# A state-space scan in a two-layer decoder trunk: VectorE leaves the odd states of six rows incomplete, and TensorE adds what they lack in a second readout

## The reference, cut to what matters

```python
def _s5_glu(h, a_re, a_im, log_dt, b_re, b_im, c_re, c_im, d_skip, w_glu):
    ...
    bu = jnp.einsum('bsgc,gpc->bsgp', u.astype(jnp.complex64), B_bar)
    a = jnp.broadcast_to(A_bar, bu.shape)
    ...
    _, states = lax.associative_scan(combine, (a, bu), axis=1)
    y = jnp.einsum('bsgp,gcp->bsgc', states, C_mat).real.reshape(B, S, D)
    y = y + d_skip.astype(f32) * h.astype(f32)
    z = jax.nn.gelu(y).astype(h.dtype)
    val, gate = jnp.split(z @ w_glu, 2, axis=-1)
    return val * jax.nn.sigmoid(gate)
```

## Time and profile before

| what | us |
|---|---|
| three runs | 2299.93, 8127.71, 2298.12; median 2299.93 |
| the profiled execution | 2300.47 |
| its span, first to last instruction | 2298.7 |
| TensorE busy | 2257.9 |
| VectorE busy | 1681.7 |
| ScalarE busy | 1031.0 |
| serial part of the mixer with TensorE idle, longest wait | 6.90 |

### The profile page before, as it was taken

One profiled execution on the slowest core, in us unless ns is written; L12 is line 12 of the kernel. 1 busy time (PEld: TensorE's weight loads), 2 busy tenths in 40 slices (PEclk: granted clock), 3 DMA queues, 4 the chain that ended last, 5 costly groups with the idle time before them and its releaser, 6 DMA issues.

```text
span 2298.7 us, 34669 instructions
## 1 busy us (share of the span) xinstructions
PE 2257.9 (98%) x11966; PEld 1875.8 (82%) x11966; DVE 1681.7 (73%) x2549; ACT 1031.0 (45%) x1158; POOL 226.3 (10%) x324
## 2 busy tenths in 40 slices
PE   9999999999999999999998899999999999999997
PEld 7888888888888888888777788888888888888886
DVE  5685758778889878788889766676677654577666
ACT  4445546444444334444342544644455433444442
POOL 1000069701111111000100000000000000000000
PEclk9999999999999999999999899999999999999999
DMA  7655365678787777666765455665665665566664
GB/s 246 200 181 180 102 231 176 215 251 270 258 270 237 254 246 234 223 223 217 256 247 185 141 193 194 214 227 192 199 191 187 200 194 194 196 189 193 194 192 137
DMA packets 134490, 478.49 MB, mean 208 GB/s; under 512 B 15968, under 2 KB 19296, under 8 KB 133232
## 3 DMA queue, kind: packets, MB, share of 16 engines
q1 hardware_dynamic: 120432, 427.35, 56.4%
q0 software_dynamic: 13808, 49.64, 6.9%
q10 hardware_dynamic: 144, 0.07, 0.0%
HBM read 457.85 MB, written 19.14 MB: 208 GB/s over the span
## 4 chain that ended last, share of the span: by engine, by line
PE 92%; DVE 5%; issue 1%; DMA 1%; ACT 0%; POOL 0%; SPq 0%; DVEq 0%; ACTq 0%
PE ps L389 29%; PE ps L390 29%; PE ps L391 29%; DMA s_bt_raw<-in_s_bt 1%; PE ps L766 1%; PE ps L742 1%; PE ps L433 1%; DVE w_lo L1155 1%; PE ps L405 0%; PE ps L403 0%; PE ps L404 0%; DVE gated L1569 0%; DVE gated L1864 0%; DVE scan_wide L1917 0%; DMA res<-in_x 0%
## 5 line engine op out<-in xcount | busy, mean ns | idle before, releaser
L1155 DVE TENSOR_TENSOR w_lo<-raw,w_hi 128x1024 fp32r<-128x1024 f32 x771 | 945.5, 1232 | 506.9 <-ACT w_hi L809 500.4
L809 ACT ACTIVATE w_hi<-raw 128x1024 fp32r<-128x1024 f32 x771 | 813.3, 1059 | 967.8 <-PE ps L391 835.6
L389 PE MATMUL ps<-w_hi,x_hi 128*128 128x512 f32 x2304 | 901.6, 391 | 2.0 <-DVE x_lo L1989 1.8
L391 PE MATMUL ps<-w_hi,x_lo 128*128 128x512 f32 x2304 | 897.8, 390 | 0.0
L390 PE MATMUL ps<-w_lo,x_hi 128*128 128x512 f32 x2304 | 897.5, 390 | 0.0
L389 PEld LDWEIGHTS ps<-w_hi,x_hi 128*128 128x128 f32 x2304 | 433.0, 188 | 92.3 <-issue 2.8
L391 PEld LDWEIGHTS ps<-w_hi,x_lo 128*128 128x128 f32 x2304 | 433.0, 188 | 90.9
L390 PEld LDWEIGHTS ps<-w_lo,x_hi 128*128 128x128 f32 x2304 | 433.2, 188 | 88.5
L389 PE MATMUL ps<-w_hi,hid_hi 128*128 128x512 f32 x656 | 256.8, 391 | 1.8 <-DVE w_lo L1155 1.7
L390 PE MATMUL ps<-w_lo,hid_hi 128*128 128x512 f32 x656 | 255.5, 389 | 0.0
L391 PE MATMUL ps<-w_hi,hid_lo 128*128 128x512 f32 x656 | 255.3, 389 | 0.0
(11 more groups left out here) (302 smaller groups left out, 1426.7 us busy)
## 6 DMA issues: line engine op xcount, KB each, us to landing
raw<-in_w_inA SPq DMA_DIRECT2D x192, 512.0 KB, 4.3
raw<-in_w_inB SPq DMA_DIRECT2D x160, 512.0 KB, 4.1
raw<-in_w_outA SPq DMA_DIRECT2D x96, 512.0 KB, 3.5
raw<-in_w_outB SPq DMA_DIRECT2D x80, 512.0 KB, 4.1
raw<-in_w_in SPq DMA_DIRECT2D x64, 512.0 KB, 4.4
raw<-in_w_gate SPq DMA_DIRECT2D x64, 512.0 KB, 3.5
raw<-in_w_glu SPq DMA_DIRECT2D x64, 512.0 KB, 3.6
raw<-in_w_out SPq DMA_DIRECT2D x32, 512.0 KB, 3.3
```

The costliest lines, as they stand in the source:

```text
L389: pe.matmul(o, hi[:, kt + k, cols], WH[:, s, k, 0:width], start=(kt + k == 0), stop=False)
L391: last = pe.matmul(o, lo[:, kt + k, cols], WH[:, s, k, 0:width], start=False, stop=(kt + k == depth - 1))
L809: act.activation(WH[:, s, :, 0:width], RAW[:, s, :, 0:width], ACT.Copy).then_inc(hi_ready, 1)
L1155: dve.tensor_tensor(WL[:, s, :, 0:width], RAW[:, s, :, 0:width], WH[:, s, :, 0:width].bitcast(F32), ALU.subtract).then_inc(lo_ready, 1)
```

## The change

For rows 0 to 5 the third step of `grow` is dropped. The second step, which summed the two parts in place, writes its sum to a buffer of its own instead, `odd_carry` (`ODD`, 31 slots x 8 numbers for each of six rows). `read_out` of such a row no longer waits for `grown` before its 32 calls; it waits for the even states alone, reads `states` out with the odd slots as they are, then waits for the row's sum in `odd_carry`, and makes 32 further calls with the same tables, 31 columns each, which add into every second column of the row's place in PSUM from the fourth slot on. Rows 6 to 15 are as before. `odd_carry` lies at offset 184 KB, where the table `s_k` lies. A new semaphore, `direct_done`, is therefore raised by the last matmul of L754, and VectorE waits for it ahead of the first pair. `grown_before(pair)` gives the new count: four steps for each of the first three pairs, six for the others.

```diff
+        ODD = at("odd_carry", [P, 6, 2, 4, SLOTS // 2 - 1], 184)
...
+        def grown_before(pair):
+
+            return 4 * min(pair, 3) + 6 * max(pair - 3, 0)
...
+            last.then_inc(direct_done, 1)
 
             def read_out(row):
 
                 pe.wait_ge(ts_in[row % 14], 32 if 2 <= row < 14 else 48 if row < 2 else 64)
-                pe.wait_ge(grown, 6 * (row // 2) + 5 + row % 2)
+                carried = row < 6
                 pe.wait_ge(even_out, row + 1)
+                if not carried:
+                    pe.wait_ge(grown, grown_before(row // 2) + 5 + row % 2)
                 for s in range(SUB):
                     for ri in range(2):
                         for a in range(4):
                             last = pe.matmul(outputs(row, a, s, s + 1), TS[row % 14][:, a, ri, PW * s:PW * (s + 1)],
-                                             ST[:, row, ri, a, :], start=False, stop=(ri == 1), skip_group_check=True)
+                                             ST[:, row, ri, a, :], start=False, stop=(ri == 1 and not carried), skip_group_check=True)
+                if carried:
+                    pe.wait_ge(grown, grown_before(row // 2) + 3 + row % 2)
+                    for s in range(SUB):
+                        for ri in range(2):
+                            for a in range(4):
+                                last = pe.matmul(outputs(row, a, s, s + 1)[:, 3:SLOTS:2], TS[row % 14][:, a, ri, PW * s:PW * (s + 1)],
+                                                 ODD[:, row, ri, a, :], start=False, stop=(ri == 1), skip_group_check=True)
                 last.then_inc(y_done, 1)
...
+                elif n_ == 1 and row < 6:
+                    w = wide[row % 2]
+                    ins = dve.tensor_tensor(ODD[:, row], w[:, :, 0], w[:, :, 1], ALU.add)
                 elif n_ == 1:
                     ins = total(row)
...
             def grow_pair(p_):
 
-                for n_ in range(3):
+                for n_ in range(2 if p_ < 3 else 3):
                     grow(2 * p_, n_)
                     grow(2 * p_ + 1, n_)
...
             fill_fours(0)
+            dve.wait_ge(direct_done, 1)
             for b in range(8):
                 grow_pair(b)
                 if b in (1, 2, 3):
-                    dve.wait_ge(grown, 6 * (b + 1))
+                    dve.wait_ge(grown, grown_before(b + 1))
                     fill_fours(b)
```

More of the change, by code:

```diff
@@ L212, in build @@
         first_half, half_scalars = sem("first_half"), sem("half_scalars")
+        direct_done = sem("direct_done")
         first_half0, var_set0, root0, scalars0, norm_half = sem("first_half0"), sem("var_set0"), sem("root0"), sem("scalars0"), sem("norm_half")
@@ L753, in _ @@
                         rows = slice(PW * a, PW * (a + 1))
-                        pe.matmul(outputs(row, a, lag, SUB), KTAB[rows, tile_of(row), lag, :],
-                                  UT[rows, row, 0:SUB - lag, :].rearrange("p s n -> p (s n)"),
-                                  start=(row % 2 == 0 and lag == 0), stop=False, skip_group_check=True)
+                        last = pe.matmul(outputs(row, a, lag, SUB), KTAB[rows, tile_of(row), lag, :],
+                                         UT[rows, row, 0:SUB - lag, :].rearrange("p s n -> p (s n)"),
+                                         start=(row % 2 == 0 and lag == 0), stop=False, skip_group_check=True)
+            last.then_inc(direct_done, 1)
             def read_out(row):
                 pe.wait_ge(ts_in[row % 14], 32 if 2 <= row < 14 else 48 if row < 2 else 64)
-                pe.wait_ge(grown, 6 * (row // 2) + 5 + row % 2)
+                carried = row < 6
                 pe.wait_ge(even_out, row + 1)
+                if not carried:
+                    pe.wait_ge(grown, grown_before(row // 2) + 5 + row % 2)
                 for s in range(SUB):
@@ L1894, in grow @@
             def grow(row, n_):
-                done = 6 * (row // 2) + 2 * n_ + row % 2
+                done = grown_before(row // 2) + 2 * n_ + row % 2
                 if done >= 2:
```

## The result

| | before | with the change |
|---|---|---|
| median | 2299.61 us (18 runs) | 2303.72 us (18 runs) |
| lowest | 2296.73 us | 2300.33 us |
| profiled execution | 2300.47 us | 2301.92 us |

The ratio is 1.0019, 95% interval 1.0013 to 1.0025: slower by 3 to 6 us. The forecast was 2299.2 us, a gain of 0.7, in a range up to 2302.6. The loss is far inside 2%, but it is clear of noise, has the other sign and lies outside the range. The 18 runs before include the one of 8127.71 us, which moves their median hardly at all.

What follows compares the result with a forecast made beforehand. TensorE was taken as the bound (busy 2257.9 of 2298.7 us), so only its waits could give. VectorE's additions -0.66, clock -0.5 and row 5 +0.44 made -0.7 us: 2299.2 us from 2299.93, range 2296.3 to 2302.6.

Steps and rivals of the forecast that it cites:

- the loop through the three engines: End of the S5 scan: TensorE finishing row 2 sets, through ScalarE then VectorE, when `x_lo` 0 comes, at 1273.06.
- The early start: Row 0's 64-column calls start once its even states are out, at 1259.0 in place of 1261.27: 2.27 us earlier.
- The second readout: The further 31-column calls of rows 0 to 5: 0.82 us a row at 1.2 GHz, 0.44 at 2.4.
- When TensorE finishes row 2: Rows 0 to 2: the early start is eaten by 2.5 us of second readouts; an earlier full clock leaves 0.5 us gained.
- Rows 3 and 4 "cost nothing": Their second readouts lie in TensorE's idle 2.85 and 1.81 us; at most 0.44 to 0.82 each if `x_lo` came earlier.
- The second term: Row 2 on TensorE: full clock returns sooner, bringing its end forward by 0.7 to 1.1 us; half taken, -0.5 us.
- the rival by which the full clock returns early: Chunk 0 on TensorE: full clock returns before it and stays; total -2.5 us, 2297.4 us; chance 0.2.
- The third term: Row 5, behind chunk 0: its second readout is on the path, +0.44 us at full clock, +0.82 at half; 0.44 taken.
- instructions run out: TensorE's instruction queue: 384 more matmuls and as many weight loads bring one more stop, +1.4 us, 2301.3 us; chance 0.15.
- short calls cost like long ones: Second readouts: 31 columns cost what 64 do, 1.69 us at half clock; +1.9 us taken, 2301.8 us; chance 0.15.
- nothing arrives: Clock moves as before, row 2 isn't earlier, -0.66 is met by +0.44 to +0.82; 2299.9 us; chance 0.2.
- VectorE's -0.66 us: Pair 2 on VectorE: its dropped additions, behind the wait for row 4, bring `x_lo` 0 forward by 0.66 us.

Runs made afterwards that it cites:

- e2: The changed kernel with 8 columns a call in the second readout in place of 31, as many calls: 2305.49 us, 1.0026 of the kernel before.
- e3: The changed kernel with 64 dense columns a call in the second readout in place of 31, as many calls: 2303.97 us, 1.0019 of the kernel before.
- e4: The changed kernel with 16 calls a row in the second readout in place of 32: 2296.87 us, 0.9983 of the kernel before.
- e5: The changed kernel with only row 0 read out in two goes, rows 1 to 5 as before: 2297.34 us, 0.9988 of the kernel before.
- e9: The kernel before with 32 calls of L754 cut in two, 128 instructions more, same columns and sums: 2297.67 us, 0.9987 of the kernel before.

## Why the prediction was wrong, point by point

- **What bounds the kernel, and the loop through the three engines: right.** The end of row 2 sets `x_hi` 0, row 4's even states and `x_lo` 0. The loss travelled on this way: 1.8 us at `x_hi` 0, 1.1 at `x_lo` 0 and at chunk 0, 2.1 at chunk 1 behind row 5's second readout, 2.3 at chunk 5.
- **The early start: right.** The first readout began 2.2 us sooner against the even states, 2.27 forecast.
- **The second readout, 0.82 us at half clock and 0.44 at full: mis-sized.** It took 0.88 (1259.80 to 1260.68) and 0.59. I carried the proportion between 128 and 64 columns down to 31, and it ends in between: 8 columns cost what 31 do (e2). The Trainium skill's rule (TensorEngine Tiling (Array Packing), Instruction Overhead), that few columns cost what about 60 do, fits 8 against 31; 31 against 64 it doesn't, 0.59 to 0.89. The mis-sizing alone would have been 0.06 to 0.15 us a row.
- **The step that failed: "When TensorE finishes row 2".** I summed the work of the calls, 1.69 + 0.82 a row, as if the instructions were always there. From row 1's stop on a row took 3.3 to 3.6 us, of which TensorE worked 1.5 at full clock. Row 2 ended 1.8 us later than before against the even states, not 0.5 sooner. e2, e3 and e4 show that the number of instructions sets this, and the pieces' transfers that TensorE stood until the next one had come.
- **Rows 3 and 4 "cost nothing": wrong too, by the same step.** Their idle time was there only if TensorE ran ahead of VectorE. Row 4's second readout ended just as chunk 0 began.
- **The second term, -0.5 us by the clock: right in that the clock rose sooner, wrong in its worth, which was nil.** In the profile the clock rose near 1261, 3 us after the first readout and not 5.0 to 5.9, and stayed up to 1274.6. But at full clock TensorE reaches the end of a piece sooner and stands longer. What the clock gives, the supply takes. So the rival by which the full clock returns early had its rise, without the gain; the clock then fell as chunk 0 began (0.50 from 1274.7 to 1278.0).
- **The third term, row 5, +0.44: too small.** 0.59 for the calls and then 1.20 of "issue" in row 6, on the path. Chunk 0 gave 0.9 us back, 4.5 us to the next readout in place of 5.4, as the clock rose before its end.
- **Rival "instructions run out": the right mechanism, the wrong count.** I gave it 0.15 and one stop. I took it for a rare event, since I had counted two stops in the trace, and not the instructions ahead of them: rows 13 to 15 are a dense run at full clock, and it stopped after 190 matmuls and their 190 weight loads. The change makes such a run of rows 0 to 4. The objection I raised, that transfers are few there, was beside the point: the stops came at a DMA share of 0.27.
- **Rival "short calls cost like long ones"** gave 2301.8 us, the right sign and half the loss, for the wrong reason; e2 and e3 rule it out.
- **Rival "nothing arrives"** (2299.9 us) is out as well: the interval excludes it.
- **VectorE's -0.66 us and the cover of `direct_done`: right.** The last matmul of the `s_k` table ended at 1252.7 and VectorE came to its wait at 1257.3. From row 4's product to `x_lo` 0 VectorE took 4.48 us (1268.80 to 1273.28) in place of 5.14 (1267.92 to 1273.06): the first term came in full and is why 1.8 us lost at `x_hi` 0 are 1.1 at `x_lo` 0. What pairs 0 and 1 saved vanished in the wait of 4.43 us, as forecast.

## What to carry to other kernels

Before adding small matmuls, count instructions, not columns: each call here is four (two matmuls, two weight loads), and a run of them at full clock was served at about 75 in a microsecond. A trick that shortens another engine's work at the price of calls on TensorE can pay for the one row where TensorE is waiting (e5, though its gain isn't separated from the late stop's), and did not for five more behind it. And a gain or loss of one part in a thousand can come with where code falls, not with what it does: run a control that only shifts it (e9) before believing the reason.

## What the runs showed of the hardware that I had not expected

- TensorE's instructions came in pieces of 16 KB, and rows of 256 instructions followed each other at 3.3 to 3.6 us with "issue" gaps of 1.1 to 1.9 us, at a clock of 1.00. Each gap ended 2.3 to 2.5 us after a piece's transfer had begun.
- 128 more instructions ahead of a wait took a 2.14 us stop away some 60 us later, and the kernel ran at 0.9987 of the time before (0.9978 to 0.9996); with 256 more the stop was 2.14 us again, at 0.9995 (0.9986 to 1.0004).
- In blocks of 32 outputs, 64 records took 0.60 us with 8 columns, 0.59 with 31 and 0.89 with 64 at full clock.
